# Four weight slots 16 bytes further apart and a big activation buffer 16 bytes later, in a fused two-layer transformer kernel

## The reference

```python
def first_block(x, p, ...):
    u = rms_norm(h, ln_mix_pre)
    hq, hf, hi, hg, aq, ak, av = split(u @ w_in)               # 2048 x 7168
    mixed = concat(hgrn2_mixer(hq, hf, hi, hg), dilated_attention_mixer(aq, ak, av)) @ w_out
    h = h + rms_norm(mixed, ln_mix_post)
    y = conv_gated_mlp(rms_norm(h, ln_ffn_pre), w_up, conv_w, conv_b, w_down)   # 2048 x 11264, 5632 x 2048
    h = h + rms_norm(y, ln_ffn_post)
    return h + (p @ w_pe) * sigmoid(h @ w_pg)

def second_block(x, mem, ...):
    proj = rmsnorm(x, norm_g) @ w_in                           # convolution, fox attention, memory attention
    ...
    return rmsnorm(x + concat(y_conv, y_fox, y_mem) @ w_out, final_g)
```

## Time and profile before

| | us |
|---|---|
| median of 3 runs | 1770.68 |
| lowest, highest | 1770.66, 1771.2 |
| the profiled execution | 1770.93 |
| its span, first to last instruction | 1769.2 |
| TensorE busy | 1754.7 |
| VectorE busy | 1257.6 |
| ScalarE busy | 934.6 |
| GpSimd busy | 615.3 |
| memory read | 323.85 MB, 184 GB/s over the span |

### The profile page before, as it was taken

The page is one execution under the profiler, slowest core; times in us unless marked ns, Lnnn a source line. Parts: engine busy times, 40 slices in busy tenths (PEclk is TensorE's granted clock), DMA queues, the critical chain, the costliest instruction groups (busy, mean ns, idle before and its releaser), DMA issues.

```text
span 1769.2 us, 29555 instructions
## 1 busy us (share of the span) xinstructions
PE 1754.7 (99%) x10189; PEld 1541.6 (87%) x10189; DVE 1257.6 (71%) x1594; ACT 934.6 (53%) x1247; POOL 615.3 (35%) x621
## 2 busy tenths in 40 slices
PE   9999999999999999999999999999999999999997
PEld 7888888888888888888888888888888888888886
DVE  6877777665598777777777644445887788887754
ACT  5544554554476555555555433334655567775532
POOL 1743345556613333111111322221262255551032
PEclk9999999999999999999999999999999999999999
DMA  8444444436565555555555555556455444444453
GB/s 316 177 176 165 167 166 166 167 143 248 184 236 189 190 188 190 190 190 190 190 190 190 169 191 186 194 184 220 168 190 201 168 167 166 166 166 164 170 190 119
DMA packets 51153, 326.61 MB, mean 185 GB/s; under 512 B 5793, under 2 KB 6433, under 8 KB 18465
## 3 DMA queue, kind: packets, MB, share of 16 engines
q1 hardware_dynamic: 49952, 323.86, 50.8%
q10 hardware_dynamic: 1152, 2.11, 0.3%
HBM read 323.85 MB, written 2.10 MB: 184 GB/s over the span
## 4 chain that ended last, share of the span: by engine, by line
PE 97%; DVE 2%; DMA 1%; ACT 1%; issue 0%; ACTq 0%; DVEq 0%
PE ps L1849 59%; PE ps L1850 30%; PE ps_lev L1849 1%; PE ps_sc L1888 1%; PE ps_lev L1924 1%; PE ps_lev L1974 1%; PE ps_t L1878 1%; DVE wlo L996 0%; DMA x_in<-in_x_turned 0%; PE ps_lev L1850 0%; DMA stage<-in_w_b 0%; PE bank_b L1979 0%; PE bank_a L1893 0%; DVE big L1441 0%; DVE o_out L1707 0%; ACT big L794 0%
## 5 line engine op out<-in xcount | busy, mean ns | idle before, releaser
L1849 PE MATMUL ps<-act_a,whi 128*128 128x512 f32 x3056 | 1069.4, 394 | 0.1
L996 DVE TENSOR_TENSOR wlo<-stage,whi 128x2048 fp32r<-128x2048 f32 (+1 forms) x314 | 690.5, 2199 | 243.3 <-ACT whi L480 238.4
L1850 PE MATMUL ps<-act_a,wlo 128*128 128x256 f32 x3056 | 854.3, 280 | 0.0
L1849 PEld LDWEIGHTS ps<-act_a,whi 128*128 128x128 f32 x3056 | 573.6, 188 | 125.7 <-issue 1.1
L480 ACT ACTIVATE whi<-stage 128x2048 fp32r<-128x2048 f32 (+1 forms) x314 | 565.9, 1802 | 124.7 <-DMA stage<-in_w_down 105.2
L1850 PEld LDWEIGHTS ps<-act_a,wlo 128*128 128x128 f32 x3056 | 574.0, 188 | 0.4
L1849 PE MATMUL ps<-big,whi 128*128 128x512 f32 x1536 | 534.5, 392 | 0.6 <-DVE wlo L996 0.6
L1850 PE MATMUL ps<-big,wlo 128*128 128x256 f32 x1536 | 429.3, 280 | 0.0
L487 ACT ACTIVATE small<-ps 128x256 f32<-128x256 f32 x240 | 91.9, 383 | 536.4 <-PE ps L1850 536.4
L1849 PEld LDWEIGHTS ps<-big,whi 128*128 128x128 f32 x1536 | 288.3, 188 | 64.3 <-ACT pe_out L789 0.9
L1850 PEld LDWEIGHTS ps<-big,wlo 128*128 128x128 f32 x1536 | 288.4, 188 | 0.1
(11 more groups left out here) (374 smaller groups left out, 1349.2 us busy)
## 6 DMA issues: line engine op xcount, KB each, us to landing
stage<-in_w_a SPq DMA_DIRECT2D x166, 1024.0 KB, 4.8
stage<-in_w_b SPq DMA_DIRECT2D x86, 1024.0 KB, 4.8
stage<-in_w_down SPq DMA_DIRECT2D x64, 704.0 KB, 4.1
stage<-in_w_a SPq DMA_DIRECT2D x8, 256.0 KB, 8.5
mem_raw<-in_memT SPq DMA_DIRECT2D x1, 2048.0 KB, 9.3
mem_again<-in_memT SPq DMA_DIRECT2D x1, 2048.0 KB, 9.1
x_in<-in_x_turned ACTq DMA_DIRECT2D x7, 256.0 KB, 9.2
x_in<-in_xT SPq DMA_DIRECT2D x3, 512.0 KB, 5.8
```

Source lines behind the costliest of these rows:

```text
L996: dve.tensor_tensor(wlo[:, slot, part], stage[:, slot, part], whi[:, slot, part].bitcast(F32), ALU.subtract).then_inc(w_lo, 1)
L1849: pe.matmul(dst, whi[:, slot, c * P:(c + 1) * P], act, start=start, stop=False)
L1850: return pe.matmul(dst[:, T:2 * T], wlo[:, slot, c * P:(c + 1) * P], act[:, 0:T], start=False, stop=stop)
```

## The change

The slots of `stage`, `wlo` and `whi` get a pitch of 2048 + 4 numbers in place of 2048, that is 8208 bytes in place of 8192; the used part of a slot stays 2048 numbers. Each of the two regions grows by 64 bytes, so all that lies behind moves by 128. `big` gets a row 32 bytes longer and starts 16 bytes into it. `big_at`, from which the scratch tiles are counted, is the start of the row plus 32 bytes; two tiles over it, `mem_raw` and `xg`, are put back to the start of the row. No instruction, wait, transfer size or order changes.

```diff
+SLOT_PAD = 4
...
-        stage = sb("stage", [P, NS, BW])
-        wlo = over("wlo", stage_at, 0, [P, NS, BW], F32R)
-        whi = sb("whi", [P, NS, BW], F32R)
+        stage = sb("stage", [P, NS, BW + SLOT_PAD])[:, :, 0:BW]
+        wlo = over("wlo", stage_at, 0, [P, NS, BW + SLOT_PAD], F32R)[:, :, 0:BW]
+        whi = sb("whi", [P, NS, BW + SLOT_PAD], F32R)[:, :, 0:BW]
...
-        big_at = at[0]
-        big = sb("big", [P, FT, 2 * T], F32R)
+        big_row = sb("big", [P, 8 + FT * 2 * T], F32R)
+        big = big_row[:, 4:4 + FT * 2 * T].rearrange("p (k t) -> p k t", t=2 * T)
+        big_at = at[0] - 4 * FT * 2 * T
...
-        mem_raw = over("mem_raw", big_at, 0, [P, KT, T])
-        xg = over("xg", big_at, 16 * KB, [P, KT, T])
+        mem_raw = over("mem_raw", big_at - 32, 0, [P, KT, T])
+        xg = over("xg", big_at - 32, 16 * KB, [P, KT, T])
```

## The result

The changed kernel takes 1782.16 us (1781.74 to 1782.33, 4 runs) against 1770.78 us, a ratio of 1.0064 with a 95% interval of 1.0051 to 1.0076: 11.4 us slower. The profiled execution took 1782.11 us with a span of 1780.3 us, 11.1 us more than before. In the changed kernel lines 1849 and 1850 are 1851 and 1852, lines 480 and 996 are 482 and 998.

A forecast was written before the change was run, and what follows sets the result against it. TensorE was taken to bound the kernel, its 4672 matmul pairs at 346.7 ns making 92% of the span. The terms summed as 0 + 0 + 0 + 0, giving 1770.7 us, with a range of 1745 to 1795.

The forecast's parts named there:

- The likeliest case: Whole kernel: the change does nothing to any read, 1770.7 us, own range 1767 to 1774; chance 0.40.
- slower by collisions: Rival: new slot relations make weight load and matmul meet more often, 5.6 ns in 3504 pairs, 1790 us; chance 0.29.
- step (a): Pace of TensorE's high and low matmul pairs, 346.7 ns: shift taken as 0, bounds +28 and -101 us.
- The list of what the change can act on: Addresses can act only on TensorE's own reads, the durations of the splitting instructions, or the transfers.
- the upper bound: Pace of a pair: at most +8 ns in the three of four slots with a new remainder, +28 us.
- The slots that should have kept their pace: Slot 0 with act_a and slot 1 with big keep remainder 32 by 64, so 346.7 ns.
- 21.7 ns of excess: Part of a pair's 346.7 ns above 325 ns, without a cause the trace names: fixed cost or colliding reads.
- faster rival: New relations avoid collisions: one slot in four gains 25 us, 1745 us, or three gain 76, 1695 us; chance 0.27.
- first part of the prediction: What bounds the kernel: TensorE's pairs; other engines' writes and transfers are not felt by a running matmul.
- (b): Splitting into high parts on ScalarE and low parts on VectorE: change 0, with 7.6 and 4.2 us of slack.
- (c): Transfers into slots at odd offsets: value 0; at most a doubled landing, just hidden by the slack.
- rival of the transfers: Packets to odd offsets land 2.5 times as long, down-stage loads 2.0 us late, 64 us, 1835 us; chance 0.04.

The follow-up runs named there:

- e5: Kernel before with slots unchanged, act_a 32 bytes further from both kinds of slots and big 64 further; 1793.28 us beside 1770.90.
- g1: Kernel before with both buffers 128 bytes further from the low slots and 96 from the high slots, slots alike; 1799.80 us, 1.0164 times the kernel before.
- e3: Kernel before with 64 bytes left free between low and high slots and 64 behind the high slots, slots alike; 1771.57 us, 0.4 us from the run beside it.
- f1: Kernel before with slots unchanged, act_a 96 bytes further from both kinds of slots and big 128 further; 1774.16 us, 3.3 us slower.
- f2: Kernel before with 64 bytes free between low and high slots, 32 behind them, 32 ahead of big; 1776.46 us, 5.6 us slower.
- e4: Changed kernel, but in blocks 95 to 154 only one cell of 16 is loaded and split, TensorE's work the same; 1781.99 us.
- f3: Kernel before with every tensor 32 bytes later, all distances as before; 1770.71 us beside 1770.89.

## Why the prediction was right, and where it was not

The measured 1782.2 us lies in the range, 1745 to 1795, and the side it is on had a chance of 0.34, less than the 0.39 of no change. The likeliest case did not come; the rival "slower by collisions" did, with 11.4 us where it was priced at 20.

**The pace, step (a).** The step that failed is the value 0. Its reason was that matmul and weight load walk past each other, so that an offset changes which columns meet and not how many. e5 and g1 show the opposite: with slots alike and another distance, a pair costs 6.6 ns more on average through the whole stage. The rows that should have weighed more were the earlier trace rows: two paces for the same triples, 117.1 and 118.7 ns, each held, spoke for rhythms and against a sum of fixed costs. (The 350 ns of the three pairs behind them is weaker: in the trace's ns they are 352, 349 and 347, a return to the usual pace.) The list of what the change can act on was right: only the reads of TensorE were touched, and the upper bound, 346.7 + 8 = 354.7 ns, holds the mean of every slot or buffer in the up and down products of every run (the highest is 354.3).

**The rival's price.** 5.6 ns in three of four slots, 4.2 ns on the average pair, measured 2.6. The single size was about right (6.4 to 7.6 ns where it hit hard), but two of four slots in the up products and one of four in the down products kept 346.7 ns. For act_a that is 2.1 ns over the four slots, for big 4.1. That the measured time lies inside the range is in part luck: the range was made wide for rivals of both signs, and the forecast itself, 1770.7 us, was missed by 11.5.

**The slots that should have kept their pace.** The prediction reckoned remainders by 64 and named slot 0 with act_a and slot 1 with big as unchanged. The first came true, 346.7 ns; the second is at 353.3. Reckoned by 128 neither is unchanged: they go from (32, 32) to (32, 96). e3 shows that this distance can hold 346.7 ns; with big in slot 1, between slots of other distances, it holds 353.3. f1 fits a repeat every 128 bytes, and e5 speaks against one every 64: big at (96, 96) takes 353.3 ns in the second block, where (32, 32) keeps 346.7 in every run that has it. The period had been chosen and not read from anything, and no row of before could give it.

**The 21.7 ns of excess and the faster rival.** The excess isn't all fixed: 340 ns, 6.7 ns less, was held for 14 pairs in the changed kernel and for 30 in f2, each time at (0, 64), one of the new relations. The faster rival's mechanism is thus real, but the same relation takes 350 or 353 ns when it is entered otherwise, and in the changed kernel the gain is rare and more than outweighed.

**The other engines, first part of the prediction.** That a running matmul does not feel the others' writes and transfers was read from the earlier trace rows, and e4 confirms it as sharply as the trace allows. The Trainium skill says in SBUF — State Buffer, under Who interferes with whom, that TensorE never waits on anyone and has independent ports for weight load and moving operand. The first half agrees with e4; the second half cannot be all, since f3 against e5 shows that the distance between those two operands alone moves the pace by 2%.

**Split and transfers, steps (b) and (c).** Right. Landing is 4.8 and 4.1 us as in the earlier trace rows, and the durations of the splitting instructions have their medians where they were (this is the changed kernel; ns min, median, max):

```profile
L482 ACT ACTIVATE whi<-stage x314: 1364/1908/1934, 28.1 to 1753.0; 128x2048 fp32r<-128x2048 f32 x125, 128x1408 fp32r<-128x1408 f32 x32
L998 DVE TENSOR_TENSOR wlo<-stage,whi x314: 1611/2292/2839, 30.1 to 1755.0; 128x2048 fp32r<-128x2048 f32 x125, 128x1408 fp32r<-128x1408 f32 x32
```

Taken by slot, the loads of `in_w_a` land after 4.79 to 4.81 us (medians), in slots 1 and 3 as in 0 and 2. A transfer to a row that begins 16 bytes off a multiple of 32 lands no later, so the rival of the transfers is out.

**What stays open.** Why the pace moves in steps of 3.33 ns, which of the two reads is held up, and what in the entry chooses the rhythm, were not shown. So the sign of a change at a given distance can be measured but not foretold from these runs. That the weight load and the moving read are the two parties rests on their distance being what counts (f3, e5, g1); no run took one of the two away. The low and high distances were never varied over the whole grid, so a better one than (32, 32) may exist, and whether the 340 ns of (0, 64) can be held through a stage by another entry was not tried.

## What to carry to other kernels

In a kernel bound by TensorE, the place of the weights relative to the moving tiles is a parameter of the pace, worth up to 1.6% of the time here, though no instruction or wait shows it: count the matmuls of one line in a fixed window before and after any edit that moves an allocation. Staggering the buffers of a ring by 16 bytes mixed fast and slow rhythms and cost 0.6%. Giving them all the same distance is no cure by itself, since a bad one (e5, g1) then slows every block and costs 1.3 to 1.6%: the distance has to be measured. Look at single blocks too, since a stage's mean can be made of two rhythms (f2: 340 and 350 ns). A tensor that is added or made longer can cost such a shift unasked, so an edit that "should be neutral" and loses 1% is to be checked for moved addresses first, by shifting back what lies behind it.

## What the runs showed that was not expected

The same two matmuls, at the same clock and with nothing else waiting, hold rhythms whose means are 340.0, 346.7, 350.0 or 353.3 ns a pair, some of them by two values in turn, such as 350 and 343, or 347 and 353. One distance, (0, 64), has been seen with 340, 350 and 353 ns, and what stood between was a stop. Others are longer, with single pairs anywhere from 340 to 361 ns and means between the steps, such as 351.1 and 352.0. With slots alike, a shift of act_a by 32 bytes costs the up products 6.6 ns a pair, while a shift of everything by 32 bytes costs nothing (346.7 ns). And taking away 94% of the transfers' rate (188 to 12 GB/s) and half of VectorE's and ScalarE's work left the mean pair at 348.93 ns to the last digit.
